# The dilated branch's maxima and sums exchanged by VectorE transposes instead of TensorE matmuls, with five smaller moves, in a one-core decoder layer

## The reference

```python
x = x + 0.5 * swiglu(rms_norm(x, ffn1_norm), ...)
h = rms_norm(x, mix_norm)
[c_q | c_kv | k_rope | q_d | k_d | v_d | g_a | g_b] = h @ w_in
y_a = MLA(c_q, c_kv, k_rope) @ w_br_mla      # 8 heads, causal, latent norms of 384 and 256
y_b = DilatedMix(q_d, k_d, v_d) @ w_br_dil   # 3 groups of 8 heads, strides 1, 4, 16
x = x + (sigmoid(g_a + b_a) * y_a + sigmoid(g_b + b_b) * y_b) @ w_out
x = x + 0.5 * swiglu(rms_norm(x, ffn2_norm), ...)
y = rms_norm(x, norm_final)
# DilatedMix: each group's attention gives out_g, its row maximum m_g and sum den_g
w = softmax over the groups of (m_g + log(den_g));  y = sum_g w_g * out_g
```

## Time and profile before

| | us |
|---|---|
| median of 3 runs | 1302.68 (1302.43 to 1305.31) |
| the profiled execution | 1302.95 |
| its span, first to last instruction | 1301.2 |
| TensorE busy | 1279.7 (98%) |
| VectorE busy | 662.1 (51%) |
| ScalarE busy | 442.4 (34%) |
| DMA | 118.87 MB, 91 GB/s on average |

### The profile page before, as it was taken

One profiled execution on the slowest core, in us unless ns is written; L12 is line 12 of the kernel. 1 busy time (PEld: TensorE's weight loads), 2 busy tenths in 40 slices (PEclk: granted clock), 3 DMA queues, 4 the chain that ended last, 5 costly groups with the idle time before them and its releaser, 6 DMA issues.

```text
span 1301.2 us, 16722 instructions
## 1 busy us (share of the span) xinstructions
PE 1279.7 (98%) x6054; PEld 1039.0 (80%) x6054; DVE 662.1 (51%) x943; ACT 442.4 (34%) x763; POOL 18.7 (1%) x36
## 2 busy tenths in 40 slices
PE   8999999999999999999999999999999999999997
PEld 6788888888887777787878878788888888888886
DVE  5654444433345677564554646676644444443322
ACT  5322222322232445343333334423433333322221
POOL 0000000000000000300000000000000000000000
PEclk9999999999999999999999999999999999999998
DMA  6342222233322122512222221123322232233331
GB/s 226 98 111 97 97 97 96 89 89 103 91 91 70 63 69 65 129 66 81 80 67 83 78 81 64 65 97 97 101 96 95 96 96 97 97 91 92 100 89 65
DMA packets 36066, 118.87 MB, mean 91 GB/s; under 512 B 4680, under 2 KB 4680, under 8 KB 36032
## 3 DMA queue, kind: packets, MB, share of 16 engines
q1 hardware_dynamic: 34416, 114.83, 27.7%
q0 software_dynamic: 1328, 3.56, 1.5%
q10 hardware_dynamic: 288, 0.03, 0.0%
HBM read 115.85 MB, written 2.55 MB: 91 GB/s over the span
## 4 chain that ended last, share of the span: by engine, by line
PE 94%; DVE 3%; ACT 1%; issue 1%; DMA 1%; SPq 0%; POOL 0%; POOLq 0%; ACTq 0%; DVEq 0%
PE bank L545 37%; PE bank L378 17%; PE bank L380 16%; PE bank L379 16%; PE bank L728 1%; PE bank L751 1%; ACT w_hi L360 1%; PE bank L649 1%; PE bank L676 1%; DVE mla_stats L1437 1%; PE bank L665 1%; PE bank L768 1%; PE bank L764 1%; DVE w_lo L365 0%; PE bank L512 0%
## 5 line engine op out<-in xcount | busy, mean ns | idle before, releaser
L365 DVE TENSOR_TENSOR w_lo<-raw,w_hi 128x1024 fp32r<-128x1024 f32 (+2 forms) x221 | 259.1, 1172 | 241.9 <-ACT w_hi L360 240.0
L360 ACT ACTIVATE w_hi<-raw 128x1024 fp32r<-128x1024 f32 (+2 forms) x221 | 224.3, 1015 | 441.5 <-PE bank L545 230.4
L545 PE MATMUL bank<-act_hi,w_hi 128*128 128x512 f32 x704 | 218.5, 392 | 3.5 <-DVE act_lo L1161 3.5
L545 PE MATMUL bank<-act_lo,w_hi 128*128 128x512 f32 x704 | 217.4, 390 | 0.0
L545 PE MATMUL bank<-act_hi,w_lo 128*128 128x512 f32 x704 | 217.1, 390 | 0.0
L378 PE MATMUL bank<-act_hi,w_hi 128*128 128x512 f32 x528 | 211.9, 401 | 2.9 <-DVE mla_vt L1430 1.5
L380 PE MATMUL bank<-act_hi,w_lo 128*128 128x512 f32 x528 | 206.2, 390 | 0.0
L379 PE MATMUL bank<-act_lo,w_hi 128*128 128x512 f32 x528 | 205.9, 390 | 0.0
L545 PEld LDWEIGHTS bank<-act_hi,w_hi 128*128 128x128 f32 x704 | 132.1, 188 | 32.6 <-DVE w_lo L365 3.9
L545 PEld LDWEIGHTS bank<-act_lo,w_hi 128*128 128x128 f32 x704 | 132.6, 188 | 27.9
L545 PEld LDWEIGHTS bank<-act_hi,w_lo 128*128 128x128 f32 x704 | 132.4, 188 | 27.7
(11 more groups left out here) (173 smaller groups left out, 1058.9 us busy)
## 6 DMA issues: line engine op xcount, KB each, us to landing
raw<-in_ffn_up SPq DMA_DIRECT2D x87, 512.0 KB, 3.4
raw<-in_w_dil SPq DMA_DIRECT2D x40, 512.0 KB, 3.4
raw<-in_ffn_down SPq DMA_DIRECT2D x32, 448.0 KB, 3.3
raw<-in_ffn_down SPq DMA_DIRECT2D x16, 512.0 KB, 3.5
raw<-in_w_mla_gates SPq DMA_DIRECT2D x8, 512.0 KB, 3.4
raw<-in_w_branches SPq DMA_DIRECT2D x8, 512.0 KB, 3.4
raw<-in_w_out SPq DMA_DIRECT2D x8, 512.0 KB, 3.4
raw<-in_w_latent SPq DMA_DIRECT2D x6, 512.0 KB, 3.4
```

The costliest lines, as they stand in the source:

```text
L360: nc.scalar.activation(w_hi[:, s % SPLIT, 0:tiles * P], raw[:, s % RAW, 0:tiles * P], ACT.Copy).then_inc(hi_ready, 1)
L365: nc.vector.tensor_tensor(w_lo[:, s % SPLIT, 0:tiles * P], raw[:, s % RAW, 0:tiles * P], w_hi[:, s % SPLIT, 0:tiles * P].bitcast(F32), ALU ...
L545: last = nc.tensor.matmul(out, w[:, s % SPLIT, tile * P:(tile + 1) * P], moving[:, row, :], start=row == 0 and w is w_hi and moving is act_hi,
```

## The change

- **Exchange.** The eight matmuls per pair, their table blocks and VectorE's masking and adding go. `fold_stats` (VectorE, q = 5) and `expand_stats` (VectorE, q = 8, ahead of the split of piece s + 9) do it with 32x32 block transposes and small copies between groups of 32 partitions. `group_weights` and `scale_probs(0)` move from q = 9 to q = 8, ahead of the take of piece 8, and ScalarE's exponential of the weights moves to q = 8 too.
- **Table.** `const[:, 0:C_FREQ]` shrinks from 1416 to 384 columns.
- **Start.** Piece 1 is issued behind x chunk 3, once chunk 0 has landed; chunks 4 to 7 each wait for the landing of one chunk later than before. Token sums and spread stand one row later each (piece 2 row 2, and piece 3 row 0; a piece has four rows).
- **Keys' norm.** Mean and root of the keys stand ahead of the split of piece s + 5 on ScalarE and VectorE; the spread stands at row 4 instead of 2 of piece 4. The rotated key's addition moves behind the first head's key and value, the query scale behind the next split.
- **One split.** In `dilated_pair` ScalarE's split of piece s + 12 stands behind unit 5's copy instead of unit 4's.
- **Tail.** Four matmuls of 512 columns into an unused bank after each of the two groups of token sums.

```diff
--- before.py
+++ after.py
...
+KEEP_WARM = 4
...
-C_IDENT, C_ONES, C_EXPAND, C_FOLD = 0, P, 2 * P, 2 * P + SEQ
-C_MOD = C_FOLD + SEQ
-C_DIV = C_MOD + BLOCKS
-C_CAUSAL = C_DIV + BLOCKS
+C_IDENT, C_ONES, C_CAUSAL = 0, P, 2 * P
 C_FREQ = C_CAUSAL + P
...
-    c[:, C_EXPAND:C_EXPAND + SEQ] = p[:, None] == j[None, :] // 4
-    c[:, C_MOD:C_MOD + BLOCKS] = p[:, None] % 4 == np.arange(4)
-
-    c[:, C_FOLD:C_FOLD + SEQ] = p[:, None] == (4 * (j % P) + j // P)[None, :] % P
-    c[:, C_DIV:C_DIV + BLOCKS] = p[:, None] // 32 == np.arange(4)
...
-        exchanged = work[:, 3, 0:6 * 4 * 2 * BLOCKS]
+        SQ = 32
+        parts = work[:, 3, 0:GROUPS * 4 * BLOCKS]
+        squares = work[:, 3, 2 * SQ:3 * SQ]
+        by_stat = work[0:SQ, 3, 4 * SQ:8 * SQ].rearrange("i (v t) -> i v t", v=BLOCKS)
+        by_token = work[0:SQ, 3, 8 * SQ:12 * SQ]
...
+            sp.wait_ge(x_loaded[0], 16)
+            load(sp, 1, 0, ffn[0][0][1], TILES)
             for k in range(HALF, KM):
-                sp.wait_ge(x_loaded[k - HALF], 16)
+                sp.wait_ge(x_loaded[k - HALF + 1], 16)
                 load_x(k)
-                if k == HALF + 1:
-                    sp.wait_ge(x_loaded[2], 16)
-                    load(sp, 1, 0, ffn[0][0][1], TILES)
             sp.wait_ge(x_loaded[HALF + 1], 16)
             load_ffn(0)
...
-                        if first and f == 0 and q == 2 and k == 1:
+                        if first and f == 0 and q == 2 and k == 2:
...
                             pe.wait_ge(const_loaded, 16)
                             pe.wait_ge(sumsq_added, KM)
                             token_sums(sumsq, bank[7]).then_inc(norm_full, 1)
-                        if first and f == 0 and q == 2 and k == 3:
...
                             spread(0, rstd_first, bank[7])
...
-                    if q == 4 and k == 2:
+                    if q == 4 and k == 4:
                         spread(2, rstd_keys, bank[4])
...
-                pe.wait_ge(dil_exp, 24 * i + 24)
-                for b in range(BLOCKS):
-                    nc.tensor.matmul(bank[7][:, b * 16:(b + 1) * 16], const[:, C_FOLD + b * P:C_FOLD + (b + 1) * P],
-                                     stats[:, :, 0, 0, :], start=True, stop=True, skip_group_check=True)
-                for b in range(BLOCKS):
-                    last = nc.tensor.matmul(bank[7][:, 64 + b * 32:96 + b * 32],
-                                            const[:, C_EXPAND + b * P:C_EXPAND + (b + 1) * P],
-                                            stats[:, :, 1:3, 1, :], start=True, stop=True, skip_group_check=True)
-                last.then_inc(stats_moved, 1)
...
+            def keep_warm():
+
+                for _ in range(KEEP_WARM):
+                    nc.tensor.matmul(bank[4][:, :], w_hi[:, 0, 0:P], hid_hi[:, 0, :], start=True, stop=True)
+
             pe.wait_ge(sumsq_added, 4 * KM + KQ + KKV - 1)
             token_sums(sumsq, bank[7], stop=False)
+            keep_warm()
             pe.wait_ge(squared, 4 * KM + KQ + KKV)
             token_sums(square, bank[7], start=False).then_inc(norm_full, 1)
+            keep_warm()
             spread(5, rstd_final, bank[6])
             spread(5, rstd_final, bank[5])
...
+                if q == 3:
+                    mean_root(2, KV_LORA, root_keys)
                 if q != 1:
                     split_hi(act, s + 2, 0, LORA_TILES if q == 4 else TILES)
...
-                if q == 3:
-                    mean_root(2, KV_LORA, root_keys)
...
+                    if q == 8:
+
+                        act.wait_ge(weight_ready, i + 1)
+                        nc.scalar.activation(weight[:, :, :], weight[:, :, :], ACT.Exp).then_inc(weight_exp, 1)
                     if q in (7, 8):
                         take_dil_values(q - 7, i)
-                act.wait_ge(weight_ready, i + 1)
-                nc.scalar.activation(weight[:, :, :], weight[:, :, :], ACT.Exp).then_inc(weight_exp, 1)
                 take_dil_values(2, i)
                 split_hi(act, s + 11, d, HALF)
                 for unit in range(8):
                     take_dil_probs(unit, i)
                     if unit == 1:
                         gate_tanh(c + e + 9, MLA_HEADS + 2 * i)
-                    if unit == 4:
+                    if unit == 5:
                         split_hi(act, s + 12, d, TILES)
...
+                if q == 3:
+                    take_mean(2, bank[4][:, 0:BLOCKS])
+                    take_root(2, root_keys, 1.0, rstd_keys)
                 if q != 1:
                     split_lo(dve, s + q + 2, 0, LORA_TILES if q == 4 else TILES)
...
-                if q == 3:
-                    take_mean(2, bank[4][:, 0:BLOCKS])
-                    take_root(2, root_keys, 1.0, rstd_keys)
                 if q == 4:
...
             take_mean(3, bank[7][:, 0:BLOCKS])
-            dve.wait_ge(chunk_taken, c + 6)
-            dve.wait_ge(own, so_far())
-            nc.vector.tensor_tensor(mla_k[low, 0, :], mla_k[low, 0, :], rotated[low, :], ALU.add).then_inc(own, one())
-            take_root(3, root_query, MLA_SCALE, query_scale)
-
-            def second_rotary_key():
+
+            def add_rotated_key():
+                dve.wait_ge(chunk_taken, c + 6)
+                dve.wait_ge(own, so_far())
+                nc.vector.tensor_tensor(mla_k[low, 0, :], mla_k[low, 0, :], rotated[low, :], ALU.add).then_inc(own, one())
                 dve.wait_ge(own, so_far())
                 nc.vector.tensor_copy(mla_k[low, 1, :], mla_k[low, 0, :]).then_inc(own, one())
...
-            take_lora(s, 0, 0, 0)
-            second_rotary_key()
+            take_lora(s, 0, 0, 0, add_rotated_key)
             split_lo(dve, s + 2, 0, LORA_TILES)
+            take_root(3, root_query, MLA_SCALE, query_scale)
...
+            def fold_stats(i):
+
+                dve.wait_ge(dil_exp, 24 * i + 8)
+                dve.wait_ge(own, so_far())
+                nc.vector.transpose(squares, stats[:, :, 0, :, :].rearrange("p t o n -> p t (o n)")).then_inc(own, one())
+                dve.wait_ge(own, so_far())
+                for u in range(BLOCKS):
+                    last = nc.vector.tensor_copy(by_stat[:, :, 8 * u:8 * u + 8],
+                                                 squares[SQ * u:SQ * (u + 1), :].rearrange("i (q v) -> i v q", v=BLOCKS))
+                last.then_inc(own, one())
+                dve.wait_ge(own, so_far())
+                nc.vector.transpose(by_token, work[0:SQ, 3, 4 * SQ:8 * SQ]).then_inc(own, one())
+                dve.wait_ge(own, so_far())
+                for b in range(BLOCKS):
+                    source = by_token.rearrange("q (v t n) -> q t v n", v=BLOCKS, t=2)[:, :, :, 2 * b:2 * b + 2]
+                    last = nc.vector.tensor_copy(
+                        stats[SQ * b:SQ * (b + 1), :, 0, 1, :].rearrange("q t (v e) -> q t v e", e=2), source)
+                last.then_inc(own, one())
+
+            def expand_stats(i):
+
+                dve.wait_ge(dil_exp, 24 * i + 24)
+                dve.wait_ge(own, so_far())
+                for b in range(BLOCKS):
+                    for t in range(2):
+                        target = by_token.rearrange("q (v t g b e) -> q b t g v e", v=BLOCKS, b=BLOCKS, t=2, g=2)
+                        last = nc.vector.tensor_copy(
+                            target[:, b, t], stats[SQ * b:SQ * (b + 1), t, 1:3, 1, :].rearrange("q g (v e) -> q g v e", e=2))
+                last.then_inc(own, one())
+                dve.wait_ge(own, so_far())
+                nc.vector.transpose(work[0:SQ, 3, 4 * SQ:8 * SQ], by_token).then_inc(own, one())
+                dve.wait_ge(own, so_far())
+                for u in range(BLOCKS):
+                    last = nc.vector.tensor_copy(squares[SQ * u:SQ * (u + 1), :].rearrange("i (q v) -> i v q", v=BLOCKS),
+                                                 by_stat[:, :, 8 * u:8 * u + 8])
+                last.then_inc(own, one())
+                dve.wait_ge(own, so_far())
+                nc.vector.transpose(stats[:, :, 1:3, 0, :], squares).then_inc(own, one())
...
             def group_weights(i):
-                dve.wait_ge(stats_moved, i + 1)
-                moved = exchanged
-                mod, div = const[:, C_MOD:C_MOD + BLOCKS], const[:, C_DIV:C_DIV + BLOCKS]
-
-                for at, n, mask in ((0, 8, div), (64, 16, mod)):
-                    size = n * 8
-                    view = "p (r k e) -> p r k e"
-                    nc.vector.tensor_tensor(
-                        moved[:, at:at + size].rearrange(view, k=BLOCKS, e=2),
-                        bank[7][:, at:at + size].rearrange(view, k=BLOCKS, e=2),
-                        mask.rearrange("p (a k e) -> p a k e", a=1, e=1).to_broadcast([P, n, BLOCKS, 2]), ALU.mult).then_inc(own, one())
-                dve.wait_ge(own, so_far())
-                for t in range(2):
-                    for e in range(2):
```

(28 more changed lines are left out.)

## The result

The changed kernel takes 1286.95 us (median of 4 executions, 1286.63 to 1287.17), the kernel before 1302.74 beside it (1302.43 to 1305.31): ratio 0.9874, 95% interval 0.9857 to 0.9891. The span of the profiled execution went from 1301.2 to 1285.3 us. That is 15.8 us by the medians and 15.9 by the spans, where 15.95 were worked out.

A forecast was written before the change was run, and what follows sets the result against it. TensorE, busy for 98% of the span, was taken to bound the kernel. Gains of 4.45 + 3.0 + 8.5 + 0 = 15.95 us from 1302.95 gave 1287.0, by the median 1286.7; forecast 1286.8 us, range 1284.0 to 1291.6.

The forecast's parts named there:

- signs of being wrong: TensorE waits for w_lo at project 9, table or sum of squares at first token sums, or weight piece 3; longer tail.
- Part 1: Start: earlier second piece gains 2.9 us and the restored clock 1.7; 4.45 us counted, ends 1.8 and 4.9.
- rule for the landing: Start: bytes ahead in the queue over its rate, then 1.05 us, put the second weight piece's landing at 9.2, taken as 9.3.
- Piece 2 lands at about 14.5: Start: with chunks 4 to 7 gated later, piece 2 lands then and GpSimd's table load goes out.
- 1.7 us for the clock: Start: 24 matmuls need 5.48 of 7.16 us; the other 1.68 are the lower clock, all regained with the shorter pause.
- Part 2: Latent stage: token_rstd wait removed, 1.9 us, and mla_vt wait at the first project, 1.1; 3.0 us, ends 2.4 and 3.3.
- Part 3: Dilated stage: exchange matmuls removed, 7.2 us, and probs_t waits, 1.3 us; 8.5 us, ends 6.5 and 8.8.
- Part 4: Tail: added matmuls fall mostly into waits, overrunning each by 0.2 to 0.3 us; taken as 0, ends 0.6 either way.
- (a): Start: the queue is the bound, so the early piece delays chunks 4 to 7 or the table; 1291.2 us, chance 0.12.
- (b): Start: the piece comes early but the clock falls all the same, 1.7 us back; 1288.5 us, chance 0.09.
- (c): Dilated stage: beyond 3.8 us per expand each pair waits for its weight piece; at 5 us 1291.6 us, chance 0.08.
- (d): Dilated stage: slower than before if the expand costs 7.8 us; at 9.5 us four pairs lose 23, 1309.6; chance 0.03.

The follow-up runs named there:

- gate: Changed kernel with the early piece 1 kept, but x chunks 4 to 7 waiting for the same landings as in the kernel before: 1286.09 us.
- u_load: Changed kernel with SP's load order of the kernel before put back, all else as changed: 1289.27 us.
- u_load_fill: As u_load, with 15 idle matmuls of 512 columns between the first and second weight piece to keep TensorE busy: 1289.44 us.
- u_norm: Changed kernel with the keys' mean and root back behind the split of piece s + 5, and the spread back at row 2 of piece 4: 1289.12 us.
- u_rot: Changed kernel with the rotated key's addition and the query root back ahead of the first head's key and value: 1288.27 us.
- b_dve: Kernel before with only the exchange, the weights' place and the small table of the change: 1295.59 us.
- u_unit: Changed kernel with ScalarE's split for the next pair back behind unit 4: 1288.68 us.
- expand3: Changed kernel with expand_stats made three times over, same values: 1306.18 us.
- table1: Changed kernel with GpSimd's table load behind the landing of piece 1 instead of piece 2: 1289.82 us.
- expand2: Changed kernel with expand_stats made twice, same values: 1290.35 us.
- u_tail: Changed kernel without the eight added matmuls of the tail: 1287.19 us.

## Why the prediction was right

The forecast was 1286.8, the result 1286.95, and the range of 1284.0 to 1291.6 held it. The mechanisms were the forecast ones in the three parts that the sum counts. That the sum came out within 0.2 us was luck: its terms missed by -0.85, +0.4, +0.1 and +0.4 us, which cancel. One of the signs of being wrong was seen, the wait for the table at the first token sums.

**Part 1, the start: 4.45 forecast, 3.60 in the traces.** The rule for the landing (bytes ahead in the queue, then 1.05 us) gave 9.3, and ScalarE's split of the piece began at 9.49; the second piece started at 12.62 against 12.4, and the lower clock was gone. The step that failed is "Piece 2 lands at about 14.5": each x chunk's gate one landing later leaves the queue less than full in between, piece 2 landed at 15.7, and the table, taken to land at 20 without a wait, at 21.54. That is 0.6 of the 0.9 us at the token sums. gate, which puts the chunks' gates back, is 0.9 us faster, 0.3 of it (by the traces) at the second piece. My upper end for the table, 1.4 us of wait, did cover it. In four of seven traces with this start there was no such wait, and the part would have been 4.0 to 4.2 us. The other error is not in the sum but under it: 1.7 us for the clock is what the trace of before held. u_load is only 2.3 us above the changed kernel by the medians, and u_load_fill the same, so the usual execution of the old start seems not to have the fall. Why the medians agree all the same was not traced. The execution on which the sum stands, 1302.95, has the fall at the start and yet lies near the lower end of the range of the kernel before, so others lost time elsewhere.

**Part 2, the latent stage: 3.0 forecast, 2.11 + 1.26 = 3.37.** Both waits went (there is none at the first project now; the 0.4 us for `mla_vt` lies 10 us behind it, and was 0.3 before), each with 0.1 to 0.2 us more than its listed length, because the restart of the stream behind a wait costs some too. u_norm and u_rot bring them back one by one, 2.2 and 1.2 us in the traces. The cover held: nothing appeared behind the moved key addition and query root. One reading was wrong without harm: two rows of a latent piece are six matmuls, 1.36 us (396.86 to 398.22 in the changed kernel), and not 2.7 us.

**Part 3, the dilated stage: 8.5 forecast, 8.56 measured,** 7.0 of it shown alone by b_dve's trace and 1.6 by u_unit's. The price per pair (1.79 us, from two gaps between the same two lines) was the best founded number of the sum. VectorE's prices were sized too low: 2.05 instead of 1.4 us for the fold, 2.35 instead of 1.9 for the expand. The transposes were as taken (0.20 us for 32 columns, 0.30 for 128), the copies were not: four copies of L1544, each reading from another group of 32 partitions, take 0.74 us, 0.19 each, while the eight of L1563, which change the group only every second time, take 0.98 us, 0.12 each. That is what the Trainium skill says (VectorE: DVE Perf Modes, "Two Vector instructions with no wait between them"), and the trace agrees: where the quadrant changes, the copy starts 0.01 us after the end of the last one, 0.17 to 0.19 us after its start; where it doesn't, 0.05 to 0.09 us after its start, with the last one still running. The slack of 1.9 us became 1.7 and still covered everything.

**Part 4, the tail: 0 forecast, 0.4 in the traces,** inside its ends of 0.6. The spreads went from 2.66 to 1.95 us, and start 0.3 us later behind the last product.

**The rivals.** (a) happened only in its small half, the late table. (b) did not happen: the pause left is 0.4 us, and the granted clock behind it 1.00. (c) did not: the expand takes 2.35 us. (d) was put too far away: by its working the change would be slower than before from 7.8 us of expand on, and the 7.3 us of expand3 (576.48 to 583.82) would cost 14 us, 1300.8. It was already at 1306.18, ratio 1.0014 to the kernel before (1.0004 to 1.0025). What fails is its price per pair, the expand less 3.8 us: a pair that waits 3.0 to 3.3 us loses 4.9 to 6.3 in the trace, because behind the wait the clock is lower too. The conclusion of the prediction did not hang on it.

## What to carry to other kernels

Where one engine is busy for 98%, a change is the sum of the gaps that it closes and the instructions that it takes from that engine; price both between starts of the same two instructions, with and without. Before moving small work to an engine that is half idle, look up which wait of the busy engine comes next behind it and how far off it is; what counts is how many instructions hop between groups of 32 partitions (0.17 us from start to start against 0.05 to 0.09), more than their elements (0.17 us for 16 elements, 0.19 for 32). And move a transfer forward together with its gates: what matters is when the last thing behind it lands.

## What the runs showed of the hardware

- Behind waits of TensorE of 3.0 to 3.8 us its clock was at the lower of the two levels in every profiled execution that has such a wait (before 0.53, b_dve 0.53 and u_load 0.57 granted from 15.4 to 19 us; all four pairs of expand3). At the start that cost 1.4 to 1.7 us, in expand3 1.9 to 3.0 us per pair with the restart. Behind single waits of 1.9 us (before, u_norm), 1.7 us (table1) and 0.8 us (expand2) it stayed at 1.00. But the length of one wait is not all of it: in the tails of before and u_tail it fell behind two waits of 0.7 us, with only short matmuls between and behind them.
- The times differ from one execution of the same program to the next: 1291.34 against 1288.06 to 1289.29 us in u_load, 1304.36 to 1308.28 in expand3. With the pause closed or filled with idle matmuls, the changed kernel and u_load_fill stayed within 0.5 us, in four executions each. But not all spread is this: u_norm and u_rot, with the pause closed, each had one execution 1.4 to 2.3 us above their others at the same mean clock of 0.998, and its cause is open.
- Tables of 0.47 MB issued on GpSimd's queue at 10 us delayed the x chunks and the weights on SP's queue by up to 3.3 us (table1), while with the same tables issued at 14 us (gate) TensorE waited neither for a table nor for the weight pieces behind them.
- VectorE's 32x32 transposes of float32 took 0.20 us for 32 columns on 128 partitions and 0.30 us for 128 columns on 32 partitions.
